# A product-key expert layer on one core: 128 tokens gathered and 128 dense, with value rows of weight zero and unused experts left out of indirect transfers

## The reference

```python
def peer(h, w_pq, sub_keys, u_tab, v_tab):
    ...
        qr = (hb @ w_pq).reshape(b, t, PEER_HEADS, 2, PEER_DKEY // 2)
        sc = jnp.einsum('bthpd,hpnd->bthpn', qr, sub_keys, preferred_element_type=jnp.float32)
        s_top, i_top = lax.top_k(sc, PEER_TOPK)
        cand = s_top[..., 0, :, None] + s_top[..., 1, None, :]
        c_top, c_pos = lax.top_k(cand.reshape(b, t, PEER_HEADS, PEER_TOPK * PEER_TOPK), PEER_TOPK)
        ...
        expert = i0 * PEER_NKEYS + i1
        g = jax.nn.softmax(c_top, axis=-1)
        u = u_tab[expert]
        a = jax.nn.gelu(jnp.einsum('bthkd,btd->bthk', u, hb, preferred_element_type=jnp.float32),
                        approximate=False)
        return jnp.einsum('bthk,bthkd->btd', (g * a).astype(v_tab.dtype), v_tab[expert])
```

## Time and profile before

| | us |
|---|---|
| three runs, median | 1663.92 |
| lowest, highest | 1663.59, 1664.06 |
| span of the profiled execution | 1663.8 |
| TensorE busy | 1644.1 (99%) |
| DVE busy | 1045.3 (63%) |
| ScalarE busy | 479.3 (29%) |
| POOL busy | 303.5 (18%) |
| moved by DMA | 569.89 MB |

### The profile page before, as it was taken

One profiled execution on the slowest core, in us unless ns is written; L12 is line 12 of the kernel. 1 busy time (PEld: TensorE's weight loads), 2 busy tenths in 40 slices (PEclk: granted clock), 3 DMA queues, 4 the chain that ended last, 5 costly groups with the idle time before them and its releaser, 6 DMA issues. The chain is left out here.

```text
span 1663.8 us, 28188 instructions
## 1 busy us (share of the span) xinstructions
PE 1644.1 (99%) x11118; PEld 1562.9 (94%) x11118; DVE 1045.3 (63%) x1745; ACT 479.3 (29%) x1227; POOL 303.5 (18%) x252
## 2 busy tenths in 40 slices
PE   8999999999999999999999899999999999999999
PEld 6768888888999999999999899999999999999998
DVE  5426695767879999668777968863444334443343
ACT  6547567646551000134433334310000000000000
POOL 1020000000004332313222222131122212222220
PEclk9999999999999999999999999999999999999999
DMA  9674446466748999999999999999999999999996
GB/s 361 222 150 130 138 138 191 145 227 206 270 156 351 423 386 402 406 372 415 391 425 400 425 404 425 424 423 423 424 424 420 420 418 425 424 424 425 416 418 236
DMA packets 107055, 569.89 MB, mean 343 GB/s; under 512 B 11280, under 2 KB 13456, under 8 KB 48208
## 3 DMA queue, kind: packets, MB, share of 16 engines
q1 hardware_dynamic: 56912, 217.27, 35.1%
q0 software_dynamic: 31792, 220.50, 32.8%
q10 hardware_dynamic: 18288, 131.36, 19.2%
HBM read 563.04 MB, written 4.46 MB: 341 GB/s over the span
## 5 line engine op out<-in xcount | busy, mean ns | idle before, releaser
L1173 DVE SCALAR_TENSOR_TENSOR acts<-late,sel,acts 128x2048 f32<-128x2048 f32 x77 | 181.1, 2352 | 247.2 <-DMA late<-in_v_tab,sel 247.1
L1565 PE MATMUL ps<-acts,late 128*128 128x160 f32 x2048 | 288.3, 300 | 0.0
L1620 PE MATMUL ps<-acts,late 128*128 (+1 forms) x2048 | 284.2, 299 | 0.0
L1620 PE MATMUL ps<-acts,raw 128*128 (+1 forms) x2048 | 283.8, 299 | 0.2
L1565 PEld LDWEIGHTS ps<-acts,late 128*128 128x128 f32 x2048 | 282.4, 191 | 0.0
L1620 PEld LDWEIGHTS ps<-acts,raw 128*128 128x128 f32 x2048 | 279.8, 190 | 1.0 <-issue 1.0
L1620 PEld LDWEIGHTS ps<-acts,late 128*128 128x128 f32 x2048 | 280.1, 190 | 0.1
L1565 PE MATMUL ps<-acts,raw 128*128 128x160 f32 x1984 | 277.6, 299 | 0.0
L1565 PEld LDWEIGHTS ps<-acts,raw 128*128 128x128 f32 x1984 | 271.8, 190 | 0.0
L849 DVE TENSOR_TENSOR w_lo<-raw,w_hi 128x512 fp32r<-128x512 f32 (+1 forms) x288 | 188.7, 682 | 130.4 <-ACT w_hi L563 128.4
L1169 DVE SCALAR_TENSOR_TENSOR late<-late,acts 128x2048 f32<-128x2048 f32 x76 | 173.3, 2289 | 34.9 <-DMA late<-in_u_rows,sel 34.7
(11 more groups left out here) (227 smaller groups left out, 1560.6 us busy)
## 6 DMA issues: line engine op xcount, KB each, us to landing
raw<-in_w_in SPq DMA_DIRECT2D x72, 512.0 KB, 3.7
late<-in_u_tab SPq DMA_DIRECT2D x33, 1024.0 KB
raw<-in_u_tab SPq DMA_DIRECT2D x32, 1024.0 KB
raw<-in_v_tab SPq DMA_DIRECT2D x32, 1024.0 KB
raw<-in_v_tab ACTq DMA_DIRECT2D x32, 1024.0 KB
late<-in_v_tab SPq DMA_DIRECT2D x32, 1024.0 KB
late<-in_v_tab ACTq DMA_DIRECT2D x32, 1024.0 KB
late<-in_u_tab ACTq DMA_DIRECT2D x31, 1024.0 KB
```

The lines of the kernel that those rows point to most:

```text
L1173: V.scalar_tensor_tensor(acc, row[n % NROW], w_sp[:, n - N_OWN:n - N_OWN + 1], acc, ALU.mult, ALU.add).then_inc(row_used, 1)
L1565: ins = mm(ps[:, q, 0:N_DN], unit[:, k * P:k * P + P], hF[:, k, :], start=k == 0, stop=k == KD - 1)
L1620: ins = mm(ps[:, pair_bank(k // 2), at:at + N_DN], ring[q][:, k * P:k * P + P], acts[:, ds(i * (4 * N_DN) + q * N_DN, N_DN)], start=first ...
```

## The change

The tokens are split into halves. Tokens 0 to 127 are gathered, with all 128 picks in both tables (256 gathers; nothing is lent, the accumulator isn't copied, and it starts as the residual itself); tokens 128 to 255 are dense (`N_DN` is 128, gate groups are 32, `FIRST_G` is 64). There are six row buffers. First-table and value rows alternate from row 48 on (`ROWS`), 58 rows are gathered before the second product's unit 8, the other 198 spread among the units.

Value rows whose weight (gate times GELU) is exactly zero get an index above the table's last row (`weigh`: the index plus 32768), and their part of the indirect transfer is left out (`bounds_check`, no error). Units 0 to 7 of the second table are still loaded whole. Units 8 to 127 become indirect transfers on POOL: ScalarE sums the absolute activations of each expert over the dense tokens (`units_used`), DVE turns zero sums into an index above the table (`list_units`), and only experts that some dense token weighs are brought. What a buffer held before stays in the parts left out, and is multiplied by zero.

```diff
@@ sizes and buffers
-    SHARE = 4
-    N_SP = P - P // SHARE
-    N_DN = SEQ - N_SP
-    NRING, NROW = 4, 5
+    N_DN = SEQ - P
+    NRING, NROW = 4, 6
...
+    V_FULL = 8
+    SKIP, LAST_ROW = 32768.0, NKEY * NKEY - 1
...
-        HEAD_ORDER = [(h + 6) % NH for h in range(NH)]
         N_AHEAD = 3
-        WEIGH_AT = NKEY - 6
-        PACE_FROM, PACE_TO = NKEY - 11, 2 * NKEY - 6
+        U_FIRST = 48
+        ROWS = [("u", n) for n in range(U_FIRST)]
+        for n in range(U_FIRST, N_PICK):
+            ROWS += [("u", n), ("v", n - U_FIRST)]
+        ROWS += [("v", n) for n in range(N_PICK - U_FIRST, N_PICK)]
+        U_LAST = [ROWS.index(("u", TOPK * h + TOPK - 1)) for h in range(NH)]
+        ROWS_U = 58
+        WEIGH_AT = {0: 100, 1: 100, 2: 125}
+        UNIT_GROUPS = [(V_FULL, 24), (24, 64), (64, NKEY)]
@@ SP
-            def v_units(i):
-                for j in range(0, NRING, 2):
-                    sp.wait_ge(unit_used, i * NRING + (NKEY + j + 1 - NRING))
-                    sp.dma_start(ring[j], io["v_tab"][ds(i * (NRING * P) + j * P, P), :]).then_inc(unit_in[j], 16)
...
+            def v_unit(u):
+                sp.wait_ge(unit_used, NKEY + u + 1 - NRING)
+                sp.dma_start(ring[u % NRING], io["v_tab"][u * P:u * P + P, :]).then_inc(unit_in[u % NRING], 16)
+            for u in (0, 2, *range(NRING, V_FULL)):
+                v_unit(u)
@@ POOL
-            def gather(n):
...
-                table = io["u_rows"] if n < N_OWN else io["v_tab"]
-                k = n % N_OWN
-                if n >= NROW:
-                    pool.wait_ge(row_used, n + 1 - NROW)
-                if n >= N_OWN:
-                    pool.wait_ge(unit_used, PACE_FROM + (n - N_OWN) * (PACE_TO - PACE_FROM) // N_OWN)
-                pool.indirect_dma_start(row[n % NROW], None, table, bass.IndirectOffsetOnAxis(ap=idx[:, k:k + 1], axis=0)).then_inc(row_in[n % NROW], 16)
...
+            def gather(r):
+
+                kind, n = ROWS[r]
...
+                if n % TOPK == 0 and kind == "v":
+                    pool.wait_ge(value_ready, n // TOPK + 1)
+                if r >= NROW:
+                    pool.wait_ge(row_used, r + 1 - NROW)
+                if kind == "u":
+                    pool.indirect_dma_start(row[r % NROW], None, io["u_rows"], bass.IndirectOffsetOnAxis(ap=idx[:, n:n + 1], axis=0)).then_inc(row_in[r % NROW], 16)
+                else:
+                    pool.indirect_dma_start(row[r % NROW], None, io["v_tab"], bass.IndirectOffsetOnAxis(ap=value_rows[:, n:n + 1], axis=0),
+                                            bounds_check=LAST_ROW, oob_is_err=False).then_inc(row_in[r % NROW], 16)
...
+            for u in range(V_FULL, NKEY):
+                for k, (first, end) in enumerate(UNIT_GROUPS):
+                    if u == first:
+                        pool.wait_ge(unit_ready, k + 1)
+                pool.wait_ge(unit_used, NKEY + u + 1 - NRING)
+                pool.indirect_dma_start(ring[u % NRING], None, io["v_tab"], bass.IndirectOffsetOnAxis(ap=unit_rows[:, u:u + 1], axis=0),
+                                        bounds_check=LAST_ROW, oob_is_err=False).then_inc(value_in[u % NRING], 16)
+                end = ROWS_U + (len(ROWS) - ROWS_U) * (u + 1 - V_FULL) // (NKEY - V_FULL)
+                gathers(done, end)
+                done = end
@@ ScalarE
-            for c in range(NKEY + 1, 2 * NKEY - NRING, 2):
-                odd_unit(c + NRING)
...
+            def units_used(first, end):
+
+                for u in range(first, end):
+                    if u >= V_FULL + 12:
+                        act.wait_ge(used_done, u - V_FULL - 11)
+                    at = P * (u % 12)
+                    nc.scalar.activation(early[:, at:at + P], acts_c[u], ACT.Abs, accum_out=used_sum[:, u:u + 1]).then_inc(used_done, 1)
@@ DVE
+            def weigh(h):
+
+                dve.wait_ge(a_done, h + 1)
+                cols = slice(TOPK * h, TOPK * h + TOPK)
+                link(V.tensor_tensor(w_sp[:, cols], a_sel[:, cols], w_sp[:, cols], ALU.mult))
+                link(V.tensor_scalar(a_sel[:, cols], w_sp[:, cols], 0.0, SKIP, ALU.is_equal, ALU.mult))
+                V.tensor_tensor(value_rows[:, cols], a_sel[:, cols], idx[:, cols], ALU.add).then_inc(value_ready, 1)
+
+            def list_units(k):
+
+                first, end = UNIT_GROUPS[k]
+                dve.wait_ge(expert_in, 16)
+                dve.wait_ge(used_done, end - V_FULL)
+                link(V.tensor_scalar(used_sum[:, first:end], used_sum[:, first:end], 0.0, SKIP, ALU.is_equal, ALU.mult))
+                V.tensor_tensor(unit_rows[:, first:end], used_sum[:, first:end], expert_no[:, first:end], ALU.add).then_inc(unit_ready, 1)
...
-                if rows_done[0] < N_OWN and c % 16 != 15:
+                if c % 8 in (1, 4, 6):
                     next_row()
...
-            for turn in range(3):
-                next_row(N_OWN + (turn + 1) * N_TURN - rows_done[0])
...
+            next_row(3)
+            list_units(0)
+            weigh(2)
+            next_row(8)
+            list_units(1)
+            next_row(14)
+            list_units(2)
+            for h in range(3, NH):
+                next_row(U_LAST[h] + 13 - rows_done[0])
+                weigh(h)
+            next_row(len(ROWS) - rows_done[0])
```

More of the change, by code:

```diff
@@ L122, in build_block @@
         rope_gain = early[:, 1408:1536].rearrange("p (f c) -> p f c", f=2)
-        diag = [early[:, P * b:P * b + P] for b in range(TT)]
-        ones = early[:, P * TT:P * TT + P]
+        diag, ones = early[:, 0:P], early[:, P:2 * P]
         rs_row = early[:, 1280:1280 + N_DN]
@@ L165, in build_block @@
         xn = [region(TT * D + D * b, D) for b in range(TT)]
[L166 to L167 removed]
+        A_HF = NKEY * N_DN
+        A_HS = A_HF + KD * N_DN
+        A_ACC = A_HS + D
+        A_ROW = A_ACC + D
+        A_SCORE = A_ROW + 2 * D
+        A_LIST = A_SCORE + TT * D
+        A_TK = NKEY * SEQ - HOT
+        assert A_LIST + 4 * NKEY <= A_TK
+        hF = region(A_HF, KD * N_DN).rearrange("p (k t) -> p k t", k=KD)
+        hs = region(A_HS, D)
+        acc = region(A_ACC, D)
+        row = [region(A_ROW + D * i, D) for i in range(2)] + [late[:, (2 + i) * D:(3 + i) * D] for i in range(4)]
+        x2 = [acc, region(A_WU, D)]
         x2n = [region(D * b, D) for b in range(TT)]
@@ L254, in build_block @@
         first_in = [sem(f"first_in{i}") for i in range(2)]
+        value_in = [sem(f"value_in{i}") for i in range(NRING)]
         row_in = [sem(f"row_in{i}") for i in range(NROW)]
@@ L504, in lend_picks @@
-            def lend_picks(h):
-                pool.wait_ge(idx_ready, N_AHEAD + h)
-                at = N_OWN + TOPK * (h % 2)
-                pool.dma_start(idx[helpers, TOPK * h:TOPK * h + TOPK], idx[lenders[h // 2], at:at + TOPK]).then_inc(idx_in, 16)
-                pool.wait_ge(idx_in, 16 * (h + 1))
-            def gathers(first, end):
-                for n in range(first, end):
-                    if n < N_OWN and n % TOPK == 0:
-                        lend_picks(n // TOPK)
-                    gather(n)
@@ new lines, in gathers @@
+            def gathers(first, end):
+                for r in range(first, end):
+                    gather(r)
+            gathers(0, NROW)
+            pool.wait_ge(score_done, 2 * NH)
+            pool.wait_ge(x2_stored, 16)
+            pool.memset(region(A_ONES, NKEY * N_DN - A_ONES), 1.0).then_inc(ones_set, 1)
+            gathers(NROW, ROWS_U)
+            done = ROWS_U
+            for u in range(V_FULL, NKEY):
[8 more added lines that the diff above has]
+                done = end
@@ L815, in _ @@
                     hot_scale(scale_after[c])
-                if c == WEIGH_AT - 2:
-                    act.wait_ge(row_used, N_OWN)
-                    nc.scalar.activation(a_sel, a_sel, ACT.Gelu).then_inc(a_done, 1)
-            for c in range(NKEY + 1, 2 * NKEY - NRING, 2):
-                odd_unit(c + NRING)
+                for h in range(NH):
+                    if c == WEIGH_AT.get(h):
+                        row_gelu(h)
+            def units_used(first, end):
[4 more added lines that the diff above has]
+                    nc.scalar.activation(early[:, at:at + P], acts_c[u], ACT.Abs, accum_out=used_sum[:, u:u + 1]).then_inc(used_done, 1)
+            act.wait_ge(applied, NKEY - FIRST_G)
+            act.wait_ge(gated, N_GRP)
+            for first, end in UNIT_GROUPS:
+                units_used(first, end)
+            for h in range(NH):
+                if h not in WEIGH_AT:
+                    row_gelu(h)
             for p in range(KD // 2):
@@ L1632, in _ @@
                 v_chunk(0, q)
-            with pe.Fori(1, NKEY // 4 - 1) as i:
+            for i in range(1, V_FULL // NRING):
+                for q in range(4):
+                    v_chunk(i, q)
+            with pe.Fori(V_FULL // NRING, NKEY // 4 - 1) as i:
                 for q in range(4):
```

226 lines of the change are left out of this document (73 added, 153 removed).

## The result

The changed kernel takes 1720.85 us (median of four runs, 1713.91 to 1725.63); the kernel before, run beside it, 1663.93 (1663.59 to 1664.06). The ratio is 1.034, 95% interval 1.031 to 1.036: **slower by 3.4%**, where the forecast of 1651 us said faster. The profiled execution has a span of 1716.3 us and a time of 1718.2.

What follows compares the result with a forecast made beforehand. It took PE and DMA as jointly bounding the old kernel, POOL with DVE the changed second product: stage start 1003 + stage 635 (467 + 120 x 1.4) + tail 13 = 1651 us, range 1575 to 1745.

Steps and rivals of the forecast that it cites:

- the limit and its mechanism: Second product: POOL together with DVE decides; a gather issued during a DVE row operation doesn't end before it; DMA near 340 GB/s.
- g: Second product: idle DVE time for each of 120 gathers beyond the 198 row operations, 1.24 to 2.48 us, taken as 1.4.
- the point where the sign turns: Second product: 1.51 us of idle DVE per extra gather, from which the kernel is slower than before.
- rival 2: Second product: POOL keeps missing its place, 1.86 us or more per extra gather; end 1706, at 2.48 us 1781; chance 0.22.
- the first product's end: First product: 128 units at 3.52 us, 32 gate groups at 0.59 and 6 of stalls, 475 us, ending at 985.
- the tightest place: First product's first half: DMA demand of 64 units and some 30 rows against 225 us; +10 us allowed in the range.
- the bytes: Second product, from the first unit gather: 55.5 units, 75 first-table rows, 77.6 value rows and 1; 219 MB, 517 us.
- the tail: After the last gather: landing about 4.5, a row 2.4, eight adds 3.4, a store 2.5; 13 us.
- the buffers' order: POOL's single order of unit and row gathers, waiting on `row_used` and `unit_used`: buffers free 10 us early, priced at nothing.
- Rival 1: Second product: bytes bound it, gathers find room between DVE's operations; end 1533 to 1568, about 1550; chance 0.13.
- Rival 3: Second product: skipping saves nothing, left-out transfers still pass the DMA engines; 335 MB, 789 us, end 1805; chance 0.07.

## Why the prediction was wrong

The forecast summed to 1003 + 635 + 13. In the profiled execution it is 1018.4 + 682.7 + 15.2 = 1716.3.

- **Right: the limit and its mechanism.** POOL and DVE together decide, the gathers end some 0.8 us after row operations, POOL is never idle beyond its 0.30 us, and DMA runs near 340 GB/s (337).
- **Wrong step: g, the idle DVE that each extra gather needs.** I took 1.4 us, between 1.24 and 2.48, and gave 1.51 as the point where the sign turns. It measures (682.7 - 467)/120 = 1.80, which is the forecast's rival 2 (1.86, 1706 us; chance 0.22). That is 48 of the 65 us missed. The reason is in the way the sum was laid out: I gave the 198 held gathers a pitch of 467/198 = 2.36 us, as where DVE runs rows back to back, and priced only the other 120. Held gathers take 2.38 + 0.31 = 2.69 us, free ones 1.29: 195 x 2.69 + 123 x 1.29 = 683. The 0.33 us more on each held gather are 64 us; spread over 120 extra ones that is 0.54 on top of their own 1.29, which makes the g of 1.8. Most of the 0.33 comes from when the gather is issued. Back to back, as in the run without unit gathers, it is issued 1.03 us into the row operation and takes 2.14 us. Here DVE waits for rows, and an operation begins at any point of a free gather or of the gap behind it; the next gather is then issued sooner, 0.81 us in, and waits longer: 2.33 (the operation) - 0.81 + 0.86 = 2.38. The rest is that even back to back the pitch was 2.14 + 0.31 = 2.45. I had put this cost of rows that come in one by one at nothing, and even took it as my argument for the lower end. The trace of before already showed long holds between single rows: of the 89 gathers of its second product 36 are held, 2.10 us in the mean and up to 3.04.
- **Wrong, smaller: the first product's end**, 999.5 instead of 985. The pace is as forecast where data is there: 2317 matmul records from 740 to 1000 us, 128 of them of gate groups (32 x 0.59 = 19 us), leave 241 us for 68.4 units, 3.52 each. But from 510 to 740 us the DMA share is 1.00 at 414 GB/s and the units come 3.84 us apart by the records (59.9 in 230 us). I had called that the tightest place and allowed 10 us in the range, none in the sum.
- **Right: the bytes.** 517.2 MB moved against 633.2 with nothing left out: 116 MB, 110.6 rows or units of 1.049 MB; the forecast's middle was 120 - 55.5 + 0.37 x 128 = 112. By the runs 55.9 units are kept, as forecast 55.5.
- **Wrong, small: the tail**, 15.2 us instead of 13. The last gather ends at 1701.2, its row's operation starts 5.3 us later (I had 4.5) and takes 2.35, the eight adds take 2.74 us together (my 0.42 each was too much: six in 2.07 are 0.35 each), and from the last add at 1711.5 to the end it is 4.8 us, where I had priced only the 2.5 from a last store's issue.
- **Right: nothing for the buffers' order.** POOL stood nowhere on `row_used` or `unit_used` in the second product, beyond the first unit: of its gaps there two are over 0.35 us, 2.3 us together.
- **Rival 1** (bytes bound, near 1550) is what the kernel becomes when DVE holds POOL less: 1584 to 1596 us, at 401 to 404 rather than 424 GB/s and with a tail bound by DVE. **Rival 3** (left-out rows cost as moved ones) is refuted by the bytes (116 MB less) and by the 238 us.

## What to carry to other kernels

Before putting transfers on GpSimd's queue, count its gathers against VectorE's two-input or double-rate SBUF operations: price a gather at its held duration for each such operation that begins while gathers are queued, since each catches the next one issued, and at its free one otherwise. A busy VectorE isn't the price; the length of one of its operations is, so cutting these in two can free the queue for 2% more VectorE time (1159 to 1186 us busy, 125 us won). And once one limit is relieved, look for stretches where the next limits still have room, and move work there.

## What the runs showed of the hardware

- A gather issued beside a two-input row operation ends 0.86 us (median) after it, and each operation holds at most one: 195 of the 196 operations that started between 1018 us and the last gather's end caught exactly one. A gather that is under way when such an operation begins isn't held (55 of 55).
- The double-rate multiplication holds a gather that has run for up to 0.45 us, to 0.12 us after its own end. Where it begins 0.50 to 0.68 us into one, the gather keeps its 0.95 to 0.99 us and the multiplication takes 1.33 to 1.51 us instead of 1.28 (ten cases).
- A row left out of an indirect transfer still is a packet: under 512 B the page counts 25937 packets with 116 MB left out and 11777 with nothing left out; the difference, 14160, is 110.6 x 128, one for each row. They cost little: 402 to 414 GB/s at a full share against 422.
- The page's "HBM read" of 628.91 MB is the same with and without rows left out; only the packets' bytes tell what moved.
- A gather with a bounds check takes 0.986 us at least, without one 0.932; with the check and nothing left out it is 0.987.
- The DMA share isn't a rate: 0.92 at 337 GB/s and 0.50 at 163 GB/s with POOL held, 1.00 at 402 with the same transfers and POOL free.
